# Places of the expert weight panels in memory, and when the loads for counts over 64 are issued

## The reference, cut to what matters

```python
g_sel = jnp.argmax(g_prob, axis=-1)                      # one group of four for each token
top_p, top_i = lax.top_k(jax.nn.softmax(e_in_group), 2)  # two of its eight experts
hid = silu(h @ w_gate[e]) * (h @ w_up[e])                # for each expert e of 32, width 256
y   = y + (hid * combine[:, e]) @ w_down[e]
x   = x + y
x   = x + sigmoid(rms_norm(x) @ w_ple_gate) * rms_norm(p @ w_ple)
```

## Time and profile before

| | |
|---|---|
| median of three runs | 2161.91 us |
| the profiled execution | 2163.06 us, its span 2161.3 us |
| TensorE busy | 2114.6 us, 98% |
| VectorE, ScalarE, POOL busy | 59%, 39%, 13% |
| bytes moved by DMA | 298.13 MB, mean 138 GB/s |
| GB/s in the last eight of 40 slices | 226 321 418 415 398 396 220 59 |
| granted clock, mean | 0.998 |

### The profile page before, as it was taken

How to read it: one execution, slowest core, us unless ns; L and a number is a source line. 1 busy time by engine, 2 the same in 40 slices (tenths; PEclk the granted TensorE clock), 3 DMA queues, 4 the chain that set the end, 5 groups by cost and what they waited for, 6 DMA issues and landing times.

```text
span 2161.3 us, 27238 instructions
## 1 busy us (share of the span) xinstructions
PE 2114.6 (98%) x10492; PEld 1594.6 (74%) x10492; DVE 1269.6 (59%) x1692; ACT 834.1 (39%) x1253; POOL 278.9 (13%) x238
## 2 busy tenths in 40 slices
PE   8999999999999999999999999999999998999998
PEld 6787888888878877888888888877878884333346
DVE  7877864555577678875655555577665454000038
ACT  5456622222253445774422222364443232222143
POOL 2334300000010064000100000010000013222220
PEclk9999999999999999999999999999999999999999
DMA  5222323223214352112332222121122158999951
GB/s 197 94 101 98 117 78 116 88 87 115 79 63 147 128 169 79 42 34 88 129 113 91 87 105 99 68 78 59 59 98 88 69 226 321 418 415 398 396 220 59
DMA packets 62478, 298.13 MB, mean 138 GB/s; under 512 B 14064, under 2 KB 14448, under 8 KB 34310
## 3 DMA queue, kind: packets, MB, share of 16 engines
q1 hardware_dynamic: 41584, 259.54, 31.4%
q0 software_dynamic: 19552, 34.55, 5.2%
q10 hardware_dynamic: 1248, 2.76, 0.3%
HBM read 326.37 MB, written 22.48 MB: 161 GB/s over the span
## 4 chain that ended last, share of the span: by engine, by line
PE 77%; DVE 10%; DMA 6%; ACT 3%; issue 2%; POOL 1%; ACTq 0%; POOLq 0%; DVEq 0%
PE psum L643 21%; PE psum L645 20%; PE psum L644 20%; PE psum L1386 4%; DMA panel<-w_m 4%; PE psum L1410 3%; PE psum L1083 2%; DVE a_lo L2078 1%; PE psum L1058 1%; DMA over_panel<-w_m,over_row 1%; DVE xc L2219 1%; ACT a_hi L1484 1%; DVE hs L2174 1%; PE psum L1195 1%; PE psum L1175 0%
## 5 line engine op out<-in xcount | busy, mean ns | idle before, releaser
L643 PE MATMUL psum<-hn_hi,a_hi 128*128 128x512 f32 (+1 forms) x1592 | 626.1, 393 | 3.1 <-DVE hn_lo L2118 1.5
L645 PE MATMUL psum<-hn_hi,a_lo 128*128 128x512 f32 (+1 forms) x1592 | 618.4, 388 | 0.0
L644 PE MATMUL psum<-hn_lo,a_hi 128*128 128x512 f32 (+1 forms) x1592 | 618.2, 388 | 0.0
L643 PEld LDWEIGHTS psum<-hn_hi,a_hi 128*128 128x128 f32 (+1 forms) x1592 | 296.9, 187 | 73.9 <-issue 7.4
L644 PEld LDWEIGHTS psum<-hn_lo,a_hi 128*128 128x128 f32 (+1 forms) x1592 | 297.1, 187 | 64.5 <-issue 2.2
L645 PEld LDWEIGHTS psum<-hn_hi,a_lo 128*128 128x128 f32 (+1 forms) x1592 | 296.9, 186 | 64.2
L2078 DVE TENSOR_TENSOR a_lo<-a_raw,a_hi 128x2048 fp32r<-128x2048 f32 (+2 forms) x109 | 249.6, 2290 | 78.1 <-ACT a_hi L1484 77.6
L1484 ACT ACTIVATE a_hi<-a_raw 128x2048 fp32r<-128x2048 f32 (+2 forms) x109 | 203.4, 1868 | 75.7 <-PE psum L645 65.6
L2162 DVE TENSOR_TENSOR h<-h,psum 128x512 f32<-128x512 f32 x176 | 119.4, 687 | 78.4 <-PE psum L645 78.4
L3063 POOL TENSOR_TENSOR sq<-sq 128x512 f32<-128x512 f32 x6 | 9.0, 1504 | 1138.7 <-ACT sq L1497 1138.7
L2990 DVE TENSOR_TENSOR xhid<-xsg,psum 128x256 f32<-128x256 f32 x24 | 10.1, 422 | 232.4 <-ACT xsg L2028 232.4
(11 more groups left out here) (530 smaller groups left out, 3297.1 us busy)
## 6 DMA issues: line engine op xcount, KB each, us to landing
a_raw<-w_a SPq DMA_DIRECT2D x116, 1024.0 KB, 5.0
panel<-w_m SPq DMA_DIRECT2D x96, 1024.0 KB
b_raw<-w_b SPq DMA_DIRECT2D x64, 512.0 KB, 3.3
q_scratch<-q_hi POOLq DMA_DIRECT2D x7, 384.0 KB
q_scratch<-qb_lo POOLq DMA_DIRECT2D x7, 384.0 KB
q_hi<-q_scratch POOLq DMA_DIRECT2D x7, 384.0 KB
q_lo<-q_scratch POOLq DMA_DIRECT2D x7, 384.0 KB
token_rows<-nat POOLq DMA_DIRECT2D x4, 512.0 KB, 5.4
```

The costliest lines, as they stand in the source:

```text
L643: pe.matmul(out, w_hi, x_hi, start=first, stop=False)
L644: pe.matmul(out, w_hi, x_lo, start=False, stop=False)
L645: return pe.matmul(out, w_lo, x_hi, start=False, stop=last)
```

## The change

The ring is numbered from 0 instead of 1, and the places are given anew:

- the four over panels lie over a_raw 0 and 1 (q even) and a_hi 0 and 1 (q odd); panels 0 and 7 over a_lo 0 and 1; panels 5, 2, 3 over b_raw, b_hi, b_lo; panels 1, 8, 4, 6 in the later area
- rows_a lies over a_hi 0 and 1, that is over the over panels of odd q; w_ple over panel 6; psq over panels 1 and 8
- of the first nine loads seven wait only for the first product of A_OUT (three before), and two for the router's panels
- load_over(0) stands right behind the gathers and waits only for its table; load_over(1) waits for four tiles of xs instead of eight; ptr comes behind both
- at the end w_ple and the first two panels of the gate (A_PG) wait for other uses, as their places now have other owners.

```diff
 def ring_at(n):
-    return (n + 1) % PANELS
+    return n % PANELS
...
-            panel = [sb(f"panel{i}", [P, WA], F32, st) for i in range(PANELS - 1)]
-            over_11 = sb("over_panel11", [P, WA], F32, st)
+            over_panel = [[None, None], [None, None]]
+            for q in range(2):
+                for half in range(2):
+                    over_panel[half][q] = sb(f"over_panel{half}{q}", [P, WA], F32, st)
+            panel = [None] * PANELS
+            for i in (0, 7, 5, 2, 3):
+                panel[i] = sb(f"panel{i}", [P, WA], F32, st)
+        with ExitStack() as st:
+            sb("under_rows_a", [P, 2, WA], F32, st)
+            rows_a = sb("rows_a", [P, NT, D], F32, st)
...
-                over_00 = sb("over_panel00", [P, WA], F32, s2)
-                over_01 = sb("over_panel01", [P, WA], F32, s2)
-                over_10 = sb("over_panel10", [P, WA], F32, s2)
-                over_panel = [[over_00, over_01], [over_10, over_11]]
+                for i in (1, 8, 4):
+                    panel[i] = sb(f"panel{i}", [P, WA], F32, s2)
                 with ExitStack() as s3:
                     w_ple = sb("w_ple", [P, 2, D], F32, s3)
-                panel.append(sb(f"panel{PANELS - 1}", [P, WA], F32, s2))
+                panel[6] = sb("panel6", [P, WA], F32, s2)
...
-            early = sorted(range(PANELS), key=lambda n: (ring_at(n) < 6, ring_at(n) < 6 and ring_at(n) % 2 == A_ROUTE % 2, n))
-            for n in early + list(range(PANELS, len(PANEL_ORDER))):
+            late = [(0, 7)[1 - A_ROUTE % 2], (0, 7)[A_ROUTE % 2]]
+            early = [n for n in range(PANELS) if n not in late]
+            for n in early + late + list(range(PANELS, len(PANEL_ORDER))):
...
-                elif ring_at(n) >= 6:
+                elif n in early:
                     sp.wait_ge(tile_ready, 2 * A_OUT + 1)
                 else:
-                    sp.wait_ge(tile_ready, 2 * A_ROUTE + (ring_at(n) % 2 == A_ROUTE % 2))
+                    sp.wait_ge(tile_ready, 2 * A_ROUTE + late.index(n))
...
-            sp.wait_ge(main_used, last[PANELS - 1])
+            sp.wait_ge(main_used, last[6])
             sp.dma_start(w_ple[:, :, :], w_p.rearrange("(k p) s -> p k s", p=P)).then_inc(b_loaded[1], 16)
-            sp.wait_ge(main_used, last[0])
+            sp.wait_ge(over_used, 6 * (XOVER // 2) - 2)
             load_a(A_PG)
-            sp.wait_ge(main_used, last[1])
             load_a(A_PG + 1)
...
+            pool.wait_ge(tables_ready, 3)
+            load_over(0)
+            pool.wait_ge(xs_first, NT)
+            pool.wait_ge(xs_second, NT)
+            load_over(1)
             pool.dma_start(ptr[:, :, :], p_t.rearrange("(k p) s -> p k s", p=P)).then_inc(table_loaded, 16)
-            pool.wait_ge(tables_ready, 3)
-            pool.wait_ge(xs_first, PAIRS // P)
-            pool.wait_ge(xs_second, PAIRS // P)
-            load_over(0)
-            load_over(1)
             pool.wait_ge(tables_ready, 5)
```

More of the change, by code:

```diff
@@ L313, in build @@
             with ExitStack() as s2:
-                over_00 = sb("over_panel00", [P, WA], F32, s2)
-                over_01 = sb("over_panel01", [P, WA], F32, s2)
-                over_10 = sb("over_panel10", [P, WA], F32, s2)
-                over_panel = [[over_00, over_01], [over_10, over_11]]
+                for i in (1, 8, 4):
+                    panel[i] = sb(f"panel{i}", [P, WA], F32, s2)
                 with ExitStack() as s3:
                     w_ple = sb("w_ple", [P, 2, D], F32, s3)
-                panel.append(sb(f"panel{PANELS - 1}", [P, WA], F32, s2))
+                panel[6] = sb("panel6", [P, WA], F32, s2)
             with ExitStack() as s2:
                 psq = sb("psq", [P, KT, S], F32, s2)
-            rows_a = sb("rows_a", [P, NT, D], F32, st)
-            sb("over_rows_a", [P, NT, D], F32, st)
+            sb("over_panels", [P, 4, WA], F32, st)
             with ExitStack() as s2:
```

## The result

The changed kernel takes 2165.94 us in the median of 21 runs (2161.88 to 2167.78); the kernel before, run beside it, 2162.60 in 21 (2160.44 to 2164.94). The ratio is 1.0013, 95% interval 1.0008 to 1.0019. A second series gave 2163.85 in 11 runs against 2162.61 in 33, ratio 1.0006 (0.9997 to 1.0015). That is still inside 0.2%, the bound put at "same", but both medians are outside the range of 2157.5 to 2163.6, and the sign is the other one. The profiled execution has a span of 2165.0 us.

A forecast was written before the change was run, and what follows sets the result against it. In the experts' stage, matmuls and the DMA panel loads feeding them were taken to run neck and neck. The terms summed to -1.3 us, from 2161.91 to 2160.6 us, with a range of 2157.5 to 2163.6.

The forecast's parts named there:

- Step 1: POOL behind the gathers: load_over(0) issues at 1799.3 in ptr's place, load_over(1) at 1803.1 after four tiles, ptr at 1805.7.
- The rule weighed: Descriptors in one DMA queue start in order but overlap, so gathers ahead of the over load lose no more than an overlap.
- the 0.04 for a loss that it didn't see: Chance of 0.04 set aside for a loss by some cause the prediction did not see.
- Rival B: Gathers, 1799 to 1805 us: over-load bytes land the last gather up to 2.5 us later, net +1.2, 2163.1; chance 0.10.
- Step 2: Start of the expert stage: both over loads are there at about 1810, so TensorE's 0.97 us wait goes.
- Step 3: Ring reloads in the expert stage: DMA comes 1.2 to 1.7 us further; gain taken as 1.3, lower end 0.97.
- rival A: Expert stage: later waits eat the early lead, summing over 7.5 us after 1820; price 0, 2161.9; chance 0.25 with another rival.
- Steps 4 to 6: Seven early panels, stores up to 1 us earlier, gathers waiting for slot_row; new numbering and places; end loads hidden: gain 0 each.
- The start value: Median of the kernel before, 2161.91 us, from which the forecast gain was subtracted.

The follow-up runs named there:

- before with spread fillers: Kernel before, with the five filler products of the router's stretch spread evenly over the turning of the tokens; 2162.72 us, ratio 1.0000.
- old order: Changed kernel with ptr right behind the gathers again and both over loads only after eight tiles of xs; 2162.01 us, ratio 0.9997.
- old places with loads after four tiles: Kernel before, with only the wait of both over loads changed, from eight tiles of xs to four; 2161.32 us, ratio 0.9993.
- loads after four tiles: Changed kernel with ptr right behind the gathers and both over loads after four tiles of xs; 2162.30 us, ratio 0.9997; again 2161.87, ratio 0.9996.

## Why the prediction was wrong, point by point

- **Step 1 (the over loads' issue) is the step that failed.** It put nothing on the two issues behind the gathers but their slots on POOL, and took VectorE's copies of tiles 2 and 3 as they stood before, at 1801.04. The first issue came at 1800.12, forecast 1799.3, and it and its twin hold up these copies by 2.7 us, to 1804.37. load_over(1), waiting for them, issued at 1806.51, forecast 1803.1, and the first up product, forecast unmoved, started 3.4 to 3.7 us late. In the sum this term was 0.
- **The rule weighed was right and did not help.** The last gathers landed after 6.4 us with 1 MB behind them in their queue, as with 0.52. What no part of the text asked is whether POOL's further issuing is felt by anyone but POOL; the 0.04 for a loss that it didn't see is where the result fell. ptr in that slot had shown only that a plain load is harmless.
- **Rival B named the right place and sign, with the wrong mechanism and price.** It let the gathers land 2.5 us late from bytes; with the bytes in POOL's queue they landed in time, and an empty load did the same harm as a full one. Net it gave +1.2; measured are +1.2 and +3.3 between the medians. That one of these is its number is luck.
- **Step 2 holds**: the 0.97 us wait went, in every version with earlier loads.
- **Step 3 was taken a little too high.** In thirteen profiles with earlier loads and no fallen clock in the stage it lasts 269.30 to 270.73 us, mean 269.9; in three with late loads (before, before with spread fillers, old order) 270.59 to 271.01, mean 270.9. That is 0.9 for 1.3: the lower end, only TensorE's own wait. The 0.3 us of lead for the ring did not show: TensorE's later waits for panels sum to 6.5 to 7.6 us in the fifteen profiles with earlier loads and to 6.5 to 7.0 in the three with late ones. The 7.6 is the first profile's, over the 7.5 named as rival A's sign, and its stage is only 0.28 us shorter; in the mean of the thirteen the lead is not given back.
- **Steps 4 to 6 hold as far as the runs show**: the stores landed earlier (median 3.8 us, 5.4 before), the gathers were released by slot_row, and places and early panels gave nothing that can be told from the scatter (old order, 2162.01; old places with loads after four tiles, 2161.32).
- **Not in the prediction at all: TensorE's clock.** Behind the hold it fell at 1804 in four of the five profiles with two or three issues and no filler there, which is worth some 1.8 us. In the first profile it fell at 1780 too, so that the rank products ran at half clock and slot_row, which waits for them, came 2.36 us later behind the stores of token_rows: VectorE's wait before it is 2.63 us, 0.70 before. That comes and goes: with the old fillers it fell there in 6 of 14 profiles, with spread ones in none of 4. The clock also parts the two series of the result: its mean is 0.996 or below in 13 of the 21 runs of the first and in 1 of the 11 of the second.
- **The start value** was low by luck: the kernel before stood at 2161.91 in three runs and at 2162.60 in 21.

The first profile adds up: front +3.71, stage -0.28, slot_row +0.52 (2.36 of clock less 1.84 by which this execution reached the stores of token_rows earlier; why it did is not shown, and other profiles of kernels with the same early panels, such as loads after four tiles, reached them as late as before, at 1779.89), 3.95 us later at the PLE product: 2079.48 against 2083.43.

**Open.** What carries the hold from POOL's issuing to tiles 2 and 3 is not shown. In every one of the 18 profiles VectorE's copy of tile 2 starts 1.52 to 1.94 us after the last indirect issue of the unbroken series ends. That holds for the kernel before too, whose last such issue is the eighth gather (1798.39), so it looks as if the gathers' own issues hold tile 2 there already; no run tests that. In the changed kernel ScalarE resumes with VectorE, in some other profiles it got its half of tile 2 earlier. The four issues after four tiles, made after a pause, held up none of tiles 5 to 7. Whether the seven early panels make the fall at 1780 likelier isn't settled either: with the old fillers it fell in 6 of 11 profiles with seven early panels and in none of 3 with three.

## What to carry to other kernels

A load that must be early need only be early enough: with the first load 3.5 us later, after a pause of POOL, the stage keeps its gain and the front loses nothing. Before an issue is moved behind another engine's critical series, ask what it does to the consumers of that series while it is being issued, and not only where its bytes go; an empty load is the cheapest test for that. Where a stretch stands idle or runs on small products, look at the granted clock row by row: here a wait of 2.2 to 3.6 us was paid for again with some 1.8 us at half clock.

## What the runs showed that was not expected

- An indirect load of 8 KB and one of 1,024 KB behind the gathers cost the same, some 1.4 us each on the copying of tiles 2 and 3; a plain load of 1,024 KB cost nothing.
- 1,024 KB behind the gathers in the same queue left the last gather at 6.4 us; from another queue, and started 1.0 us ahead of that gather, 10.0.
- Five filler products, spread and not added, took the share of runs with a mean clock of 0.997 or less from 12 of 22 to 1 of 22 in the kernel with both loads after four tiles.
